# Recurrent stage in two halves: two branch products, a gate chunk, half the recurrent gates, then the other half; second root behind two silus

## The chip, the core and the metric

The kernel runs on one core of a Trainium2 chip. The metric is the device time of one execution in microseconds; less is better. The core has five engines that run side by side, each working through its own list of instructions in order: TensorE (PE in the profile, matmuls; PEld is its weight load), ScalarE (ACT), VectorE (DVE), GpSimd (POOL) and SyncE (SP, which here only issues transfers). They meet at semaphores: an instruction can wait until a semaphore has reached a value, and everything behind it on its engine waits too. Weights come from HBM into SBUF by DMA, matmuls write into eight PSUM banks of 128x512 floats.

## The reference, cut to what matters

The program computes two transformer-like blocks over 256 tokens of width 1024. The change touches only the last mixer, a gated linear recurrence, and what surrounds it:

```python
mod = c_act @ ada_w[layer] + ada_b[layer]                  # shift, scale, gate
h = rmsnorm(x, norm_g[layer]) * (1.0 + scale) + shift
proj = h @ w_in                                            # 1024 -> 2048
xr, gate = proj[..., :1024], proj[..., 1024:]
xc = conv_b + sum(xp[:, j:j + S] * conv_w[j] for j in range(4))      # causal, 4 taps
r = sigmoid(xblk @ w_a + b_a)                              # 8 blocks of 128x128
i = sigmoid(xblk @ w_x + b_x)
log_a = -8.0 * r * softplus(-lam)
a = exp(log_a)
u = sqrt(-expm1(2.0 * log_a)) * (i * xc)
hs[t] = a[t] * hs[t - 1] + u[t]                            # the recurrence over tokens
y = (hs * silu(gate)) @ w_out
x = x + gate_of_the_layer * y                              # then the last rmsnorm
```

## The kernel before, in words

Activations lie with the 1024 features on partitions, as eight tiles of 128 features x 256 tokens; a "half" of the recurrent stage is four such tiles. Every float32 product is made of three matmuls on a high and a low part (`feature_product`, L516; `token_product`, L522).

**Weights.** `weight_stream` (L115) lists chunks in the order of use. A chunk is two units of 128x1024 floats (128x512 for `wax`, which holds the block weights of the recurrent gates). SyncE loads chunk n into one of three raw slots once VectorE has made both low parts of chunk n-3 (L425). ScalarE copies each unit to its high part (`ahead`, L938, instruction L945), VectorE subtracts to get the low part (`ahead`, L1387, instruction L1392). Six units fit in the rings, so unit v waits until TensorE has used unit v-6. `product(key)` on either engine first makes five units more than that chunk and then waits until TensorE has used the chunk. So where a call of `ahead` or `product` stands in an engine's list says when the weights of later chunks are made.

**The stage in question** begins at L903 for TensorE. Numbered by chunks, TensorE does: four branch products `xr` 0 to 3 (48 matmuls each, `columns_chunk`), the recurrent gates of the first half (`gates(0)`, 24 matmuls over four banks), gate chunk `l_gate` 0, `gates(1)`, `l_gate` 1, 2 and 3, and then the output projection `lru_o` (L652): five feature tiles of 12 matmuls of 512 columns, a `fold` (four matmuls, L562) in banks 0 and 1, and the last three tiles. The projection asks for `o_ready` before tiles 0, 2, 4 and 6.

ScalarE (L1312 to L1371): for each branch product two scalings from PSUM (L1316) and, when VectorE has done the convolution, the high part (L1324); then for each half eight sigmoids (L1340), tanh and two exps (`decay`, L1326); both square roots (L1348); four silus of the gate chunks (L1354) with the high parts of the gated result between and behind them (L1359). It loads an activation table when the function needs another one: sigmoid and tanh share one, exp, sqrt and silu have their own.

VectorE (L1948 to L2002): for each branch product six convolution steps (L1957), the low part of the branch (`xc_low`, L1942), and a `modulate` (L1422, work for the layer's gate); then for each half four scalings of the rates (L1976) and the ratio (L1980); then by quarters the input product (L1989, once per half), two scans (L1991), the product with the silu (L1997) and its low part (`o_low`, L1911), which raises `o_ready`. GpSimd multiplies the input gate with the branch (L504), once per half.

## Time and profile before

| | |
|---|---|
| median of three runs | 982.44 us (979.80 to 984.41) |
| profiled execution | 984.87 us, of which the span of the trace is 983.1 us |
| TensorE matmul busy | 840.7 us, 86% of the span |
| VectorE / ScalarE / GpSimd busy | 743.7 / 519.3 / 74.6 us |
| mean granted TensorE clock | 0.954 of full speed |

The page gives for each engine its busy time, for groups of instructions their mean duration and the idle time just before them with what ended it, and a chain of work that is followed back from the last instruction. Times within the span are counted from its start. PEclk is the granted TensorE clock: 1.00 is 2.4 GHz, 0.50 is 1.2 GHz. The recurrent stage lies between 877 and 975 us of the span.

### The profile page before, as it was taken

Reading aid. Unit: us, or ns where it says so; the run is one execution under the profiler, and the core shown is the slowest. Engines: PE = TensorE matmul, PEld = TensorE weight load, DVE = VectorE, ACT = ScalarE, POOL = GpSimd, SP = SyncE. Lnnn points to the kernel's source line nnn. Section 1 sums busy time; section 2 is a strip of 40 time slices with the busy share of each in tenths; the row PEclk is TensorE's granted clock in tenths of the full one; section 3 lists DMA queues with packets and bytes.
Section 4 is the critical chain, followed back from the end, with each engine's and each line's share of the span. In section 5 each row is a group of like instructions: output and inputs, shape, how many; then the busy total and the mean of one; then the engine's idle time right before and its main releaser. Section 6 shows DMA issues by size and latency. Waiting matters only on the chain.

```text
span 983.1 us, 14674 instructions
## 1 busy us (share of the span) xinstructions
PE 840.7 (86%) x5608; PEld 765.5 (78%) x5608; DVE 743.7 (76%) x1153; ACT 519.3 (53%) x892; POOL 74.6 (8%) x118
## 2 busy tenths in 40 slices
PE   0378797999999989996989999999499789889846
PEld 0377676999999969994788998999399668879835
DVE  3889777787878867897578876867778755779675
ACT  0345656544545475447483525544455676464962
POOL 1000010010000000004000040000100000000100
PEclk9798999999999989998999999999699899999978
DMA  8877644778788649986447899875288411556411
GB/s 330 279 241 267 227 161 153 239 239 309 266 316 303 239 146 316 378 320 208 172 150 255 301 177 323 276 254 174 87 273 304 172 43 64 176 169 220 156 75 43
DMA packets 122677, 216.29 MB, mean 220 GB/s; under 512 B 12235, under 2 KB 97975, under 8 KB 115440
## 3 DMA queue, kind: packets, MB, share of 16 engines
q1 hardware_dynamic: 106828, 134.79, 40.5%
q0 software_dynamic: 12960, 72.46, 21.7%
q10 hardware_dynamic: 2820, 8.11, 2.5%
q8 instruction: 45, 0.74, 0.3%
q14 instruction: 24, 0.20, 0.1%
HBM read 214.18 MB, written 1.15 MB: 219 GB/s over the span
## 4 chain that ended last, share of the span: by engine, by line
PE 55%; DVE 23%; ACT 11%; issue 5%; DMA 5%; SPq 0%; DVEq 0%; ACTq 0%
PE bank L518 10%; PE bank L519 10%; PE bank L520 10%; PE bank L524 6%; DVE w_lo L1392 6%; PE bank L525 6%; PE bank L526 6%; DVE modsum L1422 3%; ACT w_hi L945 2%; DMA raw<-in_mod_w 2%; DMA raw<-in_ffn_w_in 2%; PE bank L573 1%; DVE of L1422 1%; DVE kk L1957 1%; PE bank L619 1%
## 5 line engine op out<-in xcount | busy, mean ns | idle before, releaser
L1392 DVE TENSOR_TENSOR w_lo<-raw,w_hi 128x1024 fp32r<-128x1024 f32 (+2 forms) x250 | 292.6, 1207 | 105.7 <-ACT w_hi L945 105.3
L518 PE MATMUL bank<-h_hi,w_hi 128*128 128x256 f32 (+2 forms) x1184 | 340.5, 288 | 13.9 <-DVE h_lo L1545 4.9
L519 PE MATMUL bank<-h_lo,w_hi 128*128 128x256 f32 (+2 forms) x1184 | 337.8, 285 | 0.0
L520 PE MATMUL bank<-h_hi,w_lo 128*128 128x256 f32 (+2 forms) x1184 | 337.5, 285 | 0.0
L945 ACT ACTIVATE w_hi<-raw 128x1024 fp32r<-128x1024 f32 (+2 forms) x250 | 249.6, 1031 | 124.4 <-PE bank L526 48.7
L518 PEld LDWEIGHTS bank<-h_hi,w_hi 128*128 128x128 f32 (+2 forms) x1184 | 228.8, 193 | 18.8 <-issue 15.2
L519 PEld LDWEIGHTS bank<-h_lo,w_hi 128*128 128x128 f32 (+2 forms) x1184 | 228.9, 193 | 1.4 <-issue 0.5
L520 PEld LDWEIGHTS bank<-h_hi,w_lo 128*128 128x128 f32 (+2 forms) x1184 | 228.9, 193 | 0.2
L524 PE MATMUL bank<-w_hi,o_hi 128*128 128x512 f32 x312 | 125.2, 401 | 15.1 <-DVE o_lo L1911 14.0
L525 PE MATMUL bank<-w_lo,o_hi 128*128 128x512 f32 x312 | 122.6, 393 | 0.0
L526 PE MATMUL bank<-w_hi,o_lo 128*128 128x512 f32 x312 | 122.3, 392 | 0.0
L1422 DVE SCALAR_TENSOR_TENSOR modsum<-modraw,small,modsum 128x2048 f32<-128x2048 f32 (+1 forms) x38 | 81.7, 2151 | 5.1 <-DMA modraw<-in_mod_w 2.5
L524 PEld LDWEIGHTS bank<-w_hi,o_hi 128*128 128x128 f32 x312 | 59.5, 191 | 28.2 <-ACT kk L1354 14.2
L526 PEld LDWEIGHTS bank<-w_hi,o_lo 128*128 128x128 f32 x312 | 59.1, 190 | 12.8
L525 PEld LDWEIGHTS bank<-w_lo,o_hi 128*128 128x128 f32 x312 | 59.3, 190 | 11.9 <-issue 0.7
L459 POOL DMA_DIRECT2D modraw<-in_mod_w x52 | 27.9, 538 | 388.7 <-DVE modsum L1422 136.2
L1130 ACT ACTIVATE kk<-kk 128x512 f32<-128x512 f32 x22 | 13.9, 633 | 76.2 <-DVE kk L1693 76.2
L459 POOL DMA_DIRECT2D modraw<-in_ada_w x32 | 17.1, 535 | 395.9 <-DVE modsum L1422 190.5
L1422 DVE SCALAR_TENSOR_TENSOR of<-modraw,small,of 128x2048 f32<-128x2048 f32 (+1 forms) x21 | 41.9, 1995 | 3.4 <-PE bank L520 2.2
L1136 ACT ACTIVATE o_hi<-kk 128x512 fp32r<-128x512 f32 x22 | 13.9, 632 | 45.3 <-DVE kk L1697 45.3
L619 PE MATMUL bank<-cst,prob 128*128 128x128 f32 x96 | 19.6, 321 | 18.4 <-ACT prob L1094 18.4
L1125 ACT ACTIVATE kk<-bank,cols 128x256 f32<-128x256 f32 x44 | 22.4, 559 | 24.3 <-PE bank L520 24.0
(268 smaller groups left out, 1122.8 us busy)
## 6 DMA issues: line engine op xcount, KB each, us to landing
raw<-in_ffn_w_in SPq DMA_DIRECT2D x88, 512.0 KB, 6.1
modraw<-in_mod_w POOLq DMA_DIRECT2D x36, 1024.0 KB, 6.7
raw<-in_ffn_w_out SPq DMA_DIRECT2D x44, 512.0 KB, 7.3
modraw<-in_ada_w POOLq DMA_DIRECT2D x16, 1024.0 KB, 5.4
raw<-in_attn_w_in SPq DMA_DIRECT2D x26, 512.0 KB, 5.8
raw<-in_moba_w_in SPq DMA_DIRECT2D x24, 512.0 KB, 9.4
modraw<-in_mod_w POOLq DMA_DIRECT2D x16, 512.0 KB, 4.3
modraw<-in_ada_w POOLq DMA_DIRECT2D x16, 512.0 KB, 5.3
```

What stands on the lines that cost most here:

```text
L459: pool.dma_start(modraw[:, slot, at:at + src.shape[1]], src).then_inc(sem(f"mod_in{slot}"), 16)
L518: pe.matmul(dst, cut(hi(u)), a_hi, start=first, stop=False, skip_group_check=True)
L519: pe.matmul(dst, cut(hi(u)), a_lo, start=False, stop=False, skip_group_check=True)
L520: return pe.matmul(dst, cut(lo(u)), a_hi, start=False, stop=last, skip_group_check=True)
L524: pe.matmul(dst, a_hi, cut(hi(u)), start=first, stop=False, skip_group_check=True)
L525: pe.matmul(dst, a_hi, cut(lo(u)), start=False, stop=False, skip_group_check=True)
L526: return pe.matmul(dst, a_lo, cut(hi(u)), start=False, stop=last, skip_group_check=True)
L619: ins = pe.transpose(b[:, i * P:(i + 1) * P], prob[:, (g % SD) * CAUSAL + i * P:(g % SD) * CAUSAL + (i + 1) * P], ident)
L945: act.activation(hi(v), raw_unit(v), ACT.Copy).then_inc(sem("w_hi_ready"), 1)
L1125: act.activation(tiles(conv, s, s + 1), bank[0][:, t * S:(t + 1) * S], ACT.Identity, bias=cb[:, f:f + 1], scale=w2[:, 2 * FT + f:2 * FT + ...
L1392: dve.tensor_tensor(lo(v), raw_unit(v), hi(v).bitcast(F32), ALU.subtract).then_inc(sem("w_lo_ready"), 1)
L1422: ins = dve.scalar_tensor_tensor(acc, src, ck, acc, ALU.mult, ALU.add)
```

## The change

In `weight_stream` the order of the chunks becomes xr 0, xr 1, l_gate 0, wax 0, xr 2, xr 3, l_gate 1, wax 1, l_gate 2, l_gate 3. TensorE follows that order, with other banks for the gates and other waits. ScalarE and VectorE take the first half (branches 0 and 1, gates, decay, root, scans) before or between the parts of the second. On ScalarE the root of the first half now stands between branches 2 and 3, and the root of the second half behind silus 0 and 1 and two high parts, ahead of silus 2 and 3: nine table loads in the stage where there were seven. The calls of `ahead` move with it. On VectorE the scans of a half come in one go. The `fold` of the projection now also needs silu 3, since its banks are those of gate chunks 2 and 3. No instruction that computes is added or removed.

```diff
--- before.py
+++ after.py
@@ -168,13 +168,14 @@
         cols(("a_gate", m), ain, 2312 + m * 256)
     rows2("attn_o", w["attn_w_out_2"][0])
     lin = w["lru_w_in_2"][0]
-    for m in range(4):
-        cols(("xr", m), lin, m * 256)
     a_and_x = [w[f"lru_w_{name}_2"][0].rearrange("n w v -> w n v") for name in ("a", "x")]
     for i in range(2):
+        for m in (2 * i, 2 * i + 1):
+            cols(("xr", m), lin, m * 256)
+        cols(("l_gate", i), lin, 1024 + i * 256)
         out.append((("wax", i), [(src[:, 4 * i:4 * i + 4], 0) for src in a_and_x], 128))
-        for m in ((0,), (1, 2, 3))[i]:
-            cols(("l_gate", m), lin, 1024 + m * 256)
+    for m in (2, 3):
+        cols(("l_gate", m), lin, 1024 + m * 256)
     rows2("lru_o", w["lru_w_out_2"][0])
     return out
 
@@ -390,8 +391,8 @@
         turn_keys += [("l_gate", m) for m in range(4)]
         turn_of = {key: n for n, key in enumerate(turn_keys)}
 
-        gate_banks = [[(4, 5), (6, 7)], [(1, 2), (3, 4)]]
-        l_gate_banks = [0, 5, 6, 2]
+        gate_banks = [[(5, 6), (7, 1)], [(3, 5), (6, 7)]]
+        l_gate_banks = [4, 2, 0, 1]
 
         def early_slot(n):
             return raw[:, n - MODRAW, :] if n < MODRAW + RAW else vv[:, 0:2048]
@@ -660,6 +661,8 @@
                             pe.wait_ge(sem("o_ready"), ready[6 + t])
                         ins = row_block(u0 + kt, (o_hi, o_lo), kt, t, h, kt == 0, False)
                     ins.then_inc(sem("w_used"), 1)
+                if name == "lru_o":
+                    pe.wait_ge(sem("turn_read"), turn_of[("l_gate", 3)] + 1)
                 if g is not None:
                     fold(g, (0, 1), parts)
                 for kt in range(KT - TAIL, KT):
@@ -900,9 +903,6 @@
             norm_turns(5)
 
 
-            for m in range(4):
-                key = ("xr", m)
-                end_chunk(columns_chunk(key, turn(key), (h_hi, h_lo), e=None if m else 5))
             def gates(i):
                 for j in range(2):
                     u = unit0("wax", i) + j
@@ -916,18 +916,25 @@
                                               tiles(o_lo, n, n + 1), True, True)
                     ins.then_inc(sem("w_used"), 1)
 
+            for m in (0, 1):
+                key = ("xr", m)
+                end_chunk(columns_chunk(key, turn(key), (h_hi, h_lo), e=None if m else 5))
+            end_chunk(columns_chunk(("l_gate", 0), bank[l_gate_banks[0]], (h_hi, h_lo)))
             gates(0)
+            for m in (2, 3):
+                if m == 3:
+                    pe.wait_ge(sem("rg_read"), 8)
+                key = ("xr", m)
+                end_chunk(columns_chunk(key, turn(key), (h_hi, h_lo), e=None))
             pe.wait_ge(sem("turn_read"), turn_of[("xr", 0)] + 1)
-            end_chunk(columns_chunk(("l_gate", 0), bank[l_gate_banks[0]], (h_hi, h_lo)))
+            end_chunk(columns_chunk(("l_gate", 1), bank[l_gate_banks[1]], (h_hi, h_lo)))
+            pe.wait_ge(sem("turn_read"), turn_of[("xr", 1)] + 1)
+            gates(1)
             pe.wait_ge(sem("turn_read"), turn_of[("xr", 3)] + 1)
-            pe.wait_ge(sem("rg_read"), 2)
-            gates(1)
-            pe.wait_ge(sem("rg_read"), 8)
-            end_chunk(columns_chunk(("l_gate", 1), bank[l_gate_banks[1]], (h_hi, h_lo)))
             end_chunk(columns_chunk(("l_gate", 2), bank[l_gate_banks[2]], (h_hi, h_lo)))
+            end_chunk(columns_chunk(("l_gate", 3), bank[l_gate_banks[3]], (h_hi, h_lo)))
             pe.wait_ge(sem("rg_read"), 16)
-            end_chunk(columns_chunk(("l_gate", 3), bank[l_gate_banks[3]], (h_hi, h_lo)))
-            pe.wait_ge(sem("turn_read"), turn_of[("l_gate", 2)] + 1)
+            pe.wait_ge(sem("turn_read"), turn_of[("l_gate", 1)] + 1)
             out_projection("lru_o", 10)
 
 
@@ -1309,7 +1316,7 @@
             gate_bias(5)
 
 
-            for m in range(4):
+            def branch(m):
                 b = turned(("xr", m))
                 for t in range(2):
                     f = 2 * m + t
@@ -1332,7 +1339,7 @@
                 act.wait_ge(sem("decay_exp"), 2 * i + 1)
                 act.activation(tiles(qz, a, b), tiles(qz, a, b), ACT.Exp).then_inc(sem("decay_exp"), 1)
 
-            for i in range(2):
+            def gates_out(i):
                 product("wax", i)
                 for j, (dst, pb) in enumerate(((qz, "b_a"), (vv, "b_x"))):
                     for k in range(4):
@@ -1340,10 +1347,8 @@
                         act.activation(tiles(dst, n, n + 1),
                                        bank[gate_banks[i][j][k // 2]][:, (k % 2) * S:(k % 2 + 1) * S], ACT.Sigmoid,
                                        bias=pcol[pb][:, n:n + 1]).then_inc(sem("rg_read"), 1)
-                ahead(unit0("l_gate", i) + AHEAD)
-                decay(i)
-                ahead(unit0("l_gate", i) + 1 + AHEAD)
-            for i in range(2):
+
+            def input_root(i):
                 act.wait_ge(sem("ratio_ready"), i + 1)
                 act.activation(tiles(of, 4 * i, 4 * i + 4), tiles(of, 4 * i, 4 * i + 4), ACT.Sqrt,
                                scale=-1.0).then_inc(sem("input_root"), 1)
@@ -1359,13 +1364,29 @@
                 act.activation(tiles(o_hi, 2 * m, 2 * m + 2), tiles(kk, 2 * m, 2 * m + 2), ACT.Copy).then_inc(
                     sem("o_hi_ready"), 1)
 
+            branch(0)
+            branch(1)
+            ahead(unit0("l_gate", 0) + AHEAD)
+            gates_out(0)
+            decay(0)
+            branch(2)
+            input_root(0)
+            branch(3)
+            ahead(unit0("l_gate", 1) + AHEAD)
+            gates_out(1)
+            ahead(unit0("l_gate", 2) + AHEAD)
+            decay(1)
+            ahead(unit0("l_gate", 2) + 1 + AHEAD)
             gate_out(0)
             gate_out(1)
+            gated_high(0)
+            gated_high(1)
+            ahead(unit0("l_gate", 3) + AHEAD)
+            input_root(1)
             gate_out(2)
-            gated_high(0)
             gate_out(3)
-            for m in range(1, 4):
-                gated_high(m)
+            gated_high(2)
+            gated_high(3)
             sqrt_table()
             ahead(last_unit[5] + TAIL)
             rms_norm(6, 5)
@@ -1945,7 +1966,7 @@
                                   tiles(o_hi, 2 * m, 2 * m + 2).bitcast(F32), ALU.subtract).then_inc(
                                       sem("xc_ready"), 1)
 
-            for m in range(4):
+            def branch(m):
                 product("xr", m)
                 b = bank[turn_of[("xr", m)] % 4]
                 for j in (2, 1, 0):
@@ -1963,42 +1984,67 @@
                             ins.then_inc(sem("xc_full"), 1)
 
                 dve.nop().then_inc(sem("turn_read"), 1)
-                if m:
-                    xc_low(m - 1)
-                modulate(1)
-            xc_low(3)
-            for i in range(2):
-                a, b = 4 * i, 4 * i + 4
-                ahead(unit0("wax", i) + 1 + AHEAD)
+
+            def rates(i):
                 for k in range(4):
                     n = 4 * i + k
                     dve.wait_ge(sem("rg_read"), 8 * i + k + 1)
                     dve.tensor_scalar(tiles(qz, n, n + 1), tiles(qz, n, n + 1), lam8[:, n:n + 1], None,
                                       ALU.mult).then_inc(sem("rate_ready"), 1)
-                ahead(unit0("l_gate", i) + AHEAD)
+
+            def ratio(i):
+                a, b = 4 * i, 4 * i + 4
                 dve.wait_ge(sem("decay_exp"), 2 * i + 2)
                 dve.scalar_tensor_tensor(tiles(of, a, b), tiles(of, a, b), 1.0, tiles(bias, a, b), ALU.add,
                                          ALU.mult).then_inc(sem("ratio_ready"), 1)
-                ahead(unit0("l_gate", i) + 1 + AHEAD)
-            ahead(unit0("l_gate", 2) + AHEAD)
-            for m in range(4):
-                if m % 2 == 0:
-                    a, b = 2 * m, 2 * m + 4
-                    dve.wait_ge(sem("input_root"), m // 2 + 1)
-                    dve.wait_ge(sem("ix_ready"), m // 2 + 1)
-                    link(dve.tensor_tensor(tiles(vv, a, b), tiles(vv, a, b), tiles(of, a, b), ALU.mult))
-                for n in (2 * m, 2 * m + 1):
+
+            def scans(i):
+                a, b = 4 * i, 4 * i + 4
+                dve.wait_ge(sem("input_root"), i + 1)
+                dve.wait_ge(sem("ix_ready"), i + 1)
+                link(dve.tensor_tensor(tiles(vv, a, b), tiles(vv, a, b), tiles(of, a, b), ALU.mult))
+                for n in range(a, b):
                     dve.tensor_tensor_scan(tiles(bias, n, n + 1), tiles(qz, n, n + 1), tiles(vv, n, n + 1), 0.0,
                                            ALU.mult, ALU.add).then_inc(sem("scanned"), 1)
-                if m in (1, 2):
-                    ahead(unit0("l_gate", 2) + m + AHEAD)
+
+            def gated_rows(m):
                 dve.wait_ge(sem("turn_read"), turn_of[("l_gate", m)] + 1)
                 dve.wait_ge(sem("scanned"), 2 * m + 2)
                 dve.tensor_tensor(tiles(kk, 2 * m, 2 * m + 2), tiles(kk, 2 * m, 2 * m + 2),
                                   tiles(bias, 2 * m, 2 * m + 2), ALU.mult).then_inc(sem("l_gated"), 1)
-                if m:
-                    o_low(kk, m - 1, 20)
-            o_low(kk, 3, 20)
+
+            branch(0)
+            modulate(1)
+            branch(1)
+            xc_low(0)
+            modulate(1)
+            xc_low(1)
+            rates(0)
+            ahead(unit0("l_gate", 0) + 1 + AHEAD)
+            branch(2)
+            ratio(0)
+            xc_low(2)
+            modulate(1)
+            branch(3)
+            xc_low(3)
+            modulate(1)
+            scans(0)
+            ahead(unit0("l_gate", 1) + AHEAD)
+            rates(1)
+            ahead(unit0("wax", 1) + 1 + AHEAD)
+            ratio(1)
+            ahead(unit0("l_gate", 2) + AHEAD)
+            gated_rows(0)
+            gated_rows(1)
+            o_low(kk, 0, 20)
+            o_low(kk, 1, 20)
+            ahead(unit0("l_gate", 2) + 1 + AHEAD)
+            scans(1)
+            ahead(unit0("l_gate", 3) + AHEAD)
+            for m in (2, 3):
+                gated_rows(m)
+            for m in (2, 3):
+                o_low(kk, m, 20)
             out_projection("lru_o", lambda i: fold(10, (0, 1)) if i == 2 else None)
             rms_norm(6, 5)
             dve.wait_ge(sem("final_in"), 16)
```

## Rows read from the trace of the kernel before

**Rows 1.** The page: the chain that ended last, by engine.

```profile
PE 55%; DVE 23%; ACT 11%; issue 5%; DMA 5%; SPq 0%; DVEq 0%; ACTq 0%
```

**Rows 2.** Busy time by stretch; behind POOL: PEclk, DMA share, GB/s.

```profile
877.00:903.00 26.00, 25.43 (x198) 25.33 (x198) 24.35 (x42) 15.23 (x28) 1.06 (x2) 0.93 0.55 172
...
912.00:936.00 24.00, 20.67 (x168) 20.30 (x168) 16.21 (x18) 23.81 (x34) 4.83 (x2) 1.00 0.49 175
936.00:949.30 13.30, 0.00 (x0) 0.00 (x0) 7.92 (x12) 10.15 (x13) 0.00 (x0) 0.63 0.22 81
949.30:975.00 25.70, 25.59 (x100) 20.04 (x100) 18.12 (x25) 7.94 (x14) 0.00 (x0) 0.92 0.00 1
975.00:983.10 8.10, 0.00 (x0) 0.00 (x0) 4.35 (x8) 1.15 (x5) 0.00 (x0) 0.63 0.35 129
```

**Rows 3.** Waits from 877 to 950: total us, times, longest.

```profile
ACT o_hi L1324 <- DVE kk L1957: 14.1, 4, 4.0
...
DVE w_lo L1392 <- ACT w_hi L945: 9.8, 4, 5.2
```

**Rows 4.** Timeline of ScalarE: start, duration (all of them together), what, count.

```profile
911.38 1.28 ACT L1340 ACT_TABLE_LOAD   x1
912.68 1.57 ACT L1340 ACTIVATE qz<-bank,cols 128x256 f32<-128x256 f32 x4
...
915.55 1.11 ACT L945 ACTIVATE w_hi<-raw 128x1024 fp32r<-128x1024 f32 x1
916.50 1.11 ACT L1329 ACTIVATE bias<-qz 128x1024 f32<-128x1024 f32 x1
917.62 1.28 ACT L1331 ACT_TABLE_LOAD   x1
...
920.01 1.06 ACT L1333 ACTIVATE qz<-qz 128x1024 f32<-128x1024 f32 x1
920.97 2.94 ACT L945 ACTIVATE w_hi<-raw 128x1024 fp32r<-128x1024 f32 x3
...
939.18 1.09 ACT L1354 ACTIVATE kk<-bank 128x512 f32<-128x512 f32 x2
940.15 2.00 ACT L945 ACTIVATE w_hi<-raw 128x1024 fp32r<-128x1024 f32 x2
```

**Rows 5.** Timeline of VectorE, same columns.

```profile
893.52 2.94 DVE L1957 SCALAR_TENSOR_TENSOR kk<-bank,cols,kk 128x255 f32<-128x255 f32 x6
896.37 0.68 DVE L1944 TENSOR_TENSOR o_lo<-kk,o_hi 128x512 fp32r<-128x512 f32 x1
896.97 1.28 DVE L1422 SCALAR_TENSOR_TENSOR vv<-modraw,small,vv 128x1024 f32<-128x1024 f32 x1
...
916.69 2.60 DVE L1392 TENSOR_TENSOR w_lo<-raw,w_hi 128x1024 fp32r<-128x1024 f32 x1 [2.05 <-ACT w_hi L945]
...
922.24 3.49 DVE L1392 TENSOR_TENSOR w_lo<-raw,w_hi 128x1024 fp32r<-128x1024 f32 x3
...
942.39 1.22 DVE L1989 TENSOR_TENSOR vv<-vv,of 128x1024 f32<-128x1024 f32 x1
943.64 1.27 DVE L1991 TENSOR_TENSOR_SCAN bias<-qz,vv 128x256 f32<-128x256 f32 x2
945.01 0.69 DVE L1997 TENSOR_TENSOR kk<-kk,bias 128x512 f32<-128x512 f32 x1
```

**Rows 6.** TensorE at the projection's start, from the timeline.

```profile
949.36 0.77 PE L524 MATMUL bank<-w_hi,o_hi 128*128 128x512 f32 x1 [14.01 <-DVE o_lo L1911]
```

**Rows 7.** The granted clock in windows of 2 us, columns as in Rows 2.

```profile
939.00:941.00 2.00, 0.00 (x0) 0.00 (x0) 0.00 (x0) 1.99 (x4) 0.00 (x0) 0.64 0.00 0
...
951.00:953.00 2.00, 2.00 (x6) 1.52 (x6) 2.00 (x4) 0.00 (x0) 0.00 (x0) 0.50 0.00 0
953.00:955.00 2.00, 2.00 (x10) 1.66 (x9) 2.00 (x4) 0.63 (x1) 0.00 (x0) 0.95 0.00 0
```

**Rows 8.** Raw weight transfers between 845 and 983, issue to landing.

```profile
DMA to landing us min/median/max: 2.9/4.7/7.2
```

## Prediction

> **What bounds the kernel now.** I read the page's chain first, then busy time by stretch, then waits and timelines of the last 110 us. Over the whole span the chain is mostly TensorE [rows 1], but that average doesn't hold where the change is made. Four stretches are to be told apart [rows 2]. From 877 to 903 TensorE and VectorE are both full, with the branch products and convolutions. From 912 to 936 ScalarE is full (23.81 of 24.00 us). From 936.0 to 949.3 TensorE does nothing, while ScalarE is busy for 10.15 us and VectorE for 7.92. From 949.3 to 975 the projection keeps TensorE full, and 8.1 us of norm and store follow, which the change doesn't touch. The first matmul of the projection had stood idle for 14.01 us, waiting for a low part of the gated result [rows 6]. What made that late is ScalarE's list: both halves of gates, decays and roots, and only then the silus at 939.18 [rows 4]; VectorE waits for it too (9.8 us in four waits for high parts of weights [rows 3]) and makes input product, scans and gated product from 942.39 on [rows 5]. ScalarE in turn loses 14.1 us earlier, in four waits for convolutions [rows 3]. So the price of the stage is the way through ScalarE and VectorE, not TensorE's work.
>
> **What the change does with that.** No computing instruction goes or comes. The first half's gates come before branches 2 and 3, so part of ScalarE's work moves into its early waits. I lay the new lists end to end, each instruction starting when the one before it on its engine and what it waits for are done. Steps from start to start, out of the rows: ScalarE 0.95 us for a high part, 0.53 taken for a 512-wide one (an estimate, half the columns and some overhead), eight sigmoids 2.87, tanh 0.96, second exp 0.96, silu 0.49; a table load costs 1.41, that is 1.28 to 1.30 for itself and 0.1 by which the instruction ahead of it drains longer (tanh takes 1.12 to the load, where others of its size take 0.95); load and first exp take 2.39, with the drain 2.5 [rows 4]. VectorE: six convolution steps 2.87, branch low part 0.60, modulate 1.2, low part of a weight unit 1.14 (3.49 for three), input product 1.25, scan 0.60, gated product 0.60 [rows 5]. TensorE: 0.12 us for a 256-wide matmul at full clock (25.43 us x 0.93 / 198 [rows 2]), 0.23 for a 512-wide one, and twice that at half [rows 7].
>
> First half. Unit 6 is now a 512-wide one, so the second convolution ends at 895.8 instead of 896.4. VectorE then does a low part, a modulate and a low part: 898.2. The remaining 18 gate matmuls end at 900.6. ScalarE: table and sigmoids 4.3, tanh 0.96, table and exps 3.5, to 909.4; high parts 13 and 14 to 910.9. VectorE: low part 14 to 912.2, convolution to 915.1, ratio to 916.2. ScalarE: root table and root 2.4, high parts 15 and 16 to 920.2. VectorE: low part 16 and the last convolution to 924.4. ScalarE: branch high part to 925.0, four high parts (17 to 20) to 928.8.
>
> What is hidden there. VectorE now waits for the first sigmoids (902.5) before it makes low part 9, and 9 to 12 are queued behind that: TensorE stands 1.9 us in branch product 2, but that product is ready at 908 and VectorE comes to it at 912, so nothing is lost. The wait for all eight sigmoids before branch 3 is over at 904.9, three us early. GpSimd's product (L504) now overlaps low part 10, where the one beside it before took 2.60 us instead of 1.2 [rows 5]; VectorE later waits 1.9 us for high part 13, which covers the 1.4. In the second half it overlaps parts 19 and 20, ahead of a wait of 3 us for the exps. GpSimd's last two modulation transfers go out when modulates 1 and 2 are done, ahead of its products, as before. Transfers: the wax 1 chunk is sent when low part 9 is made, at 905.0; it is needed at 910.3 by high part 14. With the median landing of 4.7 us, and 0.45 to issue, that just fits; at the longest, 7.2, it costs 2.5, at the shortest nothing [rows 8]. The other transfers have over 3 us to spare.
>
> Second half. The last branch low part is there at 925.8. TensorE has stood since 920.4, for 5.4 us, in the middle of `gates(1)`. This is the first cost that before doesn't show: its long idle was 14.01 us, in which the clock fell to half some 4.3 us in (939 to 941 has 0.64), and it came back 3.9 us after the restart, in the window from 953 [rows 6, 7]. At full clock the 18 matmuls end at 928.1 and hide behind the high parts; at half they take 4.3 and end at 930.0, which costs ScalarE 1.3. The idles between 912 and 936, 3.3 us in all, brought no fall (20.67 us busy of 24.00, clock 1.00 [rows 2]). 5.4 is nearer to the 4.3 at which it fell than to that, so I take the fall: both ends, 0 and 1.3, stay in the range. From 930.0 ScalarE: table and sigmoids 4.3, high part 0.95, tanh 0.96, table and exps 3.5, high part 0.95, silu table and two silus 2.4: 943.1. Gated products and high parts of quarters 0 and 1 alternate with VectorE to 944.6, then high part 23, root table, root: 947.9. VectorE: input product 1.25, four scans 2.4, low part 23, two gated products 1.2, two low parts behind their high parts 1.4, low part 24 with its end 1.23: 956.6. TensorE begins the projection at 944.9, does tiles 0 to 3 in 10.9 and stands 0.9 for low part 24. From 956.6: tile 4 2.7, fold 1.9, last three tiles 36 x 0.2265 + 0.2 = 8.3: 969.6. Before that end was at 975.0 [rows 2]. **The sum is -5.3 us.** The same laying out, done with before's lists, ends at 974.9, so the durations carry.
>
> The two added table loads are on this way: one root load ahead of branch 3, one second silu load in place of a shared one. They are in the sum at 1.41 each. The Trainium skill, ScalarE: Activation LUTs, What ACT_TABLE_LOAD costs, has 1.28 us for the load plus 1.38 of drain, 2.66 for each switch. The trace agrees with the first and not with the second: the load at 917.62 follows a tanh that began 1.12 before [rows 4].
>
> The profiled execution took 984.87 us for a span of 983.1; less 5.3 that is 979.6. It lies 2.4 above the median of the runs, so against 982.44 the change gives **977.1 us**.
>
> **Rivals.**
> No fall of the clock before the second half of the gates: -6.6, 975.8. For it: the idle is barely over what it took to fall. Chance 0.20.
> A second fall, at the projection: TensorE stands 3.4 us ahead of it. At half for 4 us it loses 2.0, for 7 us 3.3, of which 0.9 is hidden: -4.2 to -2.9, near 978.9. For it: the earlier stall falls in the same stretch. Against: 3.4 is under 4.3. Chance 0.18.
> The wax 1 transfer lands late: up to 2.5 more, -2.8, 979.6. VectorE's waits for the first sigmoids set its start. Chance 0.08.
> A table switch costs more here than in its rows: if ScalarE ran empty for as long as the load takes (1.28 us in place of 0.1 [rows 4]), the two added ones bring 2.4 more, -2.9, 979.5. No row shows it. Chance 0.04. By the drain that the Trainium skill, ScalarE: Activation LUTs, gives, it would be this case.
> Slower: the clock stays at half through the projection. TensorE then pays 0.20 more for each of 96 matmuls of 512 columns [rows 7]; with 0.9 of slack, 31 of them eat the 5.3 and 55 make it slower by over 0.5%; all of them give +12.8, 990. Against: before, full clock was back nine matmuls after 14 us of idle. Chance 0.04.
> The hand-offs between ScalarE and VectorE cost more than before's rows (ten in the way, each some tenths), -3 to 0: near 980.5. Chance 0.10.
>
> **How the numbers follow.** The forecast, 977.1, has 0.36. A measurement of this kernel tells about 0.5% (4.9 us) from no change; the forecast is barely over that and the runs of before spread by 4.6, so it counts 0.55 to 0.45. Faster: 0.20 from the forecast, 0.17 of the first rival, 0.08 of the second and third together: 0.45. Slower: the clock rival's 0.03 and 0.02 of the hand-offs. The rest, 0.50, is no change. Range: down to the first rival with 2 us of spread between medians (973.8), up to the late ones with the same (982.0).
>
> **What would show it.** Right: the wait for `o_ready` ahead of the projection falls from 14 us to under 5; TensorE's first 512-wide matmul is near 945 and its last near 970; an idle of about 5 us inside the second gates; ScalarE with nine loads from 900 to 955; low part 24, not a low part of the result, released the fifth tile. Wrong: ScalarE idle for long ahead of `hi` of wax 1; the first matmul of the projection after 947; half clock beyond 935; a branch 3 that is done after 926.

## The result, and the profile after

| | before | changed |
|---|---|---|
| median of 8 runs each | 984.38 us (979.80 to 986.29) | 976.22 us (973.32 to 980.15) |
| ratio of the changed kernel to before | | 0.9924 (95% interval 0.9901 to 0.9948) |
| profiled execution, its span | 984.87, 983.1 us | 980.15, 978.3 us |
| stage: first branch matmul to last matmul of the projection | 877.57 to 974.96: 97.39 us | 879.49 to 970.24: 90.75 us |

The change makes the kernel faster by 7.5 us (5.1 to 9.7 by the interval), 0.8%. The forecast was 5.3 us, 977.1. Between the two profiled executions the span fell by 4.8 us, and the stage by 6.64: the changed kernel's execution came to the stage 1.92 us later, though the code ahead of it is the same. The start of the stage lies between 872.88 and 879.49 in the twelve traces of this study, so the stage's own length is the measure for small effects, and it is used in all that follows. No kernel was traced twice, so how far this length varies by itself isn't measured; differences of 0.1 or 0.2 us are not read as effects. The first rows bound that stage in the changed kernel; they are TensorE's timeline (start, duration, what, and in brackets the idle before it and what ended it):

```profile
879.49 0.36 PE L519 MATMUL bank<-h_hi,w_hi 128*128 128x256 f32 x1 [0.94 <-DVE h_lo L1566]
...
927.02 0.58 PE L519 MATMUL bank<-o_hi,w_hi 128*128 128x256 f32 x1 [4.79 <-DVE o_lo L1965]
...
944.85 0.72 PE L525 MATMUL bank<-w_hi,o_hi 128*128 128x512 f32 x1 [2.05 <-DVE o_lo L1932]
...
969.85 0.39 PE L527 MATMUL bank<-w_hi,o_lo 128*128 128x512 f32 x1
```

The 14.01 us ahead of the projection [rows 6] have become 2.05, and 4.79 stand inside the second gates, where the low part of branch 3 is waited for. Busy time by stretch, for [rows 2]:

```profile
877.00:903.00 26.00, 23.84 (x181) 23.28 (x182) 20.60 (x36) 18.39 (x30) 1.05 (x2) 0.93 0.65 202
...
912.00:936.00 24.00, 19.21 (x145) 19.01 (x144) 22.07 (x34) 17.18 (x27) 1.55 (x1) 0.86 0.48 159
...
943.00:949.00 6.00, 4.15 (x11) 3.33 (x12) 4.42 (x6) 5.68 (x7) 0.00 (x0) 0.72 0.51 175
949.00:969.50 20.50, 20.50 (x88) 16.25 (x88) 16.29 (x23) 9.53 (x16) 0.00 (x0) 1.00 0.00 1
```

The stretch without any matmul is gone. ScalarE, which was full from 912 to 936, now has slack there too (17.18 of 24.00), and VectorE carries more (22.07 us, before 16.21). The clock column has 0.93 at the start of the stage, as before, and two new falls: one in the second gates and one at the start of the projection. In windows of 2 us the first of them, which ends after 930:

```profile
924.00:926.00 2.00, 0.00 (x0) 0.00 (x0) 1.51 (x4) 0.39 (x1) 0.00 (x0) 0.61 0.63 258
926.00:928.00 2.00, 0.98 (x4) 0.98 (x5) 1.72 (x2) 2.00 (x3) 0.00 (x0) 0.50 0.00 0
928.00:930.00 2.00, 2.00 (x12) 2.00 (x11) 1.97 (x4) 2.00 (x3) 0.00 (x0) 0.50 0.00 0
930.00:932.00 2.00, 2.00 (x14) 2.00 (x14) 2.00 (x5) 1.97 (x4) 0.00 (x0) 0.69 0.00 0
```

ScalarE over the second gates and the silus, for [rows 4], with its waits for the convolutions first, for [rows 3]:

```profile
ACT o_hi L1331 <- DVE kk L1978: 13.5, 4, 3.5
...
925.61 0.63 ACT L1331 ACTIVATE o_hi<-kk 128x512 fp32r<-128x512 f32 x1 [3.24 <-DVE kk L1978]
926.15 3.88 ACT L952 ACTIVATE w_hi<-raw 128x1024 fp32r<-128x1024 f32 x4
930.05 1.28 ACT L1347 ACT_TABLE_LOAD   x1
931.35 1.57 ACT L1347 ACTIVATE qz<-bank,cols 128x256 f32<-128x256 f32 x4
...
940.70 1.28 ACT L1359 ACT_TABLE_LOAD   x1
941.99 1.09 ACT L1359 ACTIVATE kk<-bank 128x512 f32<-128x512 f32 x2
943.35 1.23 ACT L1364 ACTIVATE o_hi<-kk 128x512 fp32r<-128x512 f32 x2 [0.27 <-DVE kk L2013]
...
945.54 1.28 ACT L1353 ACT_TABLE_LOAD   x1
946.84 1.06 ACT L1353 ACTIVATE of<-of 128x1024 f32<-128x1024 f32 x1
947.91 1.28 ACT L1359 ACT_TABLE_LOAD   x1
```

To compare with the laying out of the prediction, which began at before's 877.57, take 1.92 from these times. Three things are to be seen. The four waits for convolutions are nearly as long as before (13.5 us, before 14.1). The table load at 930.05 did not wait: the last of the second gates' matmuls ended at 931.23, the load had begun ahead of the wait, and the sigmoid followed at 931.35. And the silus begin at 940.1 (941.99 - 1.92), where the prediction's list has its second silu end at 943.1 and so its first begin at 942.1. VectorE's part, for [rows 5]:

```profile
914.04 2.93 DVE L1978 SCALAR_TENSOR_TENSOR kk<-bank,cols,kk 128x255 f32<-128x255 f32 x6
...
922.65 2.94 DVE L1978 SCALAR_TENSOR_TENSOR kk<-bank,cols,kk 128x255 f32<-128x255 f32 x6
926.28 0.69 DVE L1965 TENSOR_TENSOR o_lo<-kk,o_hi 128x512 fp32r<-128x512 f32 x1 [0.69 <-ACT o_hi L1331]
...
947.92 1.23 DVE L2005 TENSOR_TENSOR vv<-vv,of 128x1024 f32<-128x1024 f32 x1 [1.49 <-ACT of L1353]
949.19 2.44 DVE L2007 TENSOR_TENSOR_SCAN bias<-qz,vv 128x256 f32<-128x256 f32 x4
...
955.26 1.22 DVE L1413 TENSOR_TENSOR w_lo<-raw,w_hi 128x1024 fp32r<-128x1024 f32 x1
```

### The profile page after: what moved, and what is told of

Read it like the earlier page. It is cut to its first block, busy times and chain, and to the rows that moved or that the text cites. A ratio compares the mean times of both kernels' runs of the same rounds, so it can differ in the third digit from the quotient of the medians.

```text
span 978.3 us, 14677 instructions
## 1 busy us (share of the span) xinstructions
PE 847.5 (87%) x5608; PEld 771.3 (79%) x5608; DVE 742.8 (76%) x1153; ACT 521.7 (53%) x894; POOL 78.0 (8%) x118
## 3 DMA queue, kind: packets, MB, share of 16 engines
q0 software_dynamic: 12960, 72.46, 21.8%
HBM read 214.18 MB, written 1.15 MB: 220 GB/s over the span
## 4 chain that ended last, share of the span: by engine, by line
PE 56%; DVE 23%; ACT 10%; issue 5%; DMA 5%; POOLq 1%; SPq 0%; ACTq 0%; DVEq 0%
PE bank L519 10%; PE bank L521 10%; PE bank L520 10%; DVE w_lo L1413 7%; PE bank L525 6%; PE bank L526 6%; PE bank L527 6%; DVE modsum L1443 3%; ACT w_hi L952 2%; DMA raw<-in_mod_w 2%; DMA raw<-in_ffn_w_in 2%; PE bank L574 1%; PE bank L620 1%; DVE of L1443 1%; PE bank L634 1%
## 5 line engine op out<-in xcount | busy, mean ns | idle before, releaser
L1413 DVE TENSOR_TENSOR w_lo<-raw,w_hi 128x1024 fp32r<-128x1024 f32 (+3 forms) x250 | 292.0, 1205 | 96.6 <-ACT w_hi L952 96.1
L952 ACT ACTIVATE w_hi<-raw 128x1024 fp32r<-128x1024 f32 (+3 forms) x250 | 249.5, 1030 | 126.7 <-PE bank L527 49.1
L527 PEld LDWEIGHTS bank<-w_hi,o_lo 128*128 128x128 f32 x312 | 59.1, 190 | 12.8
```

The lines of the kernel that those rows point to most:

```text
L527: return pe.matmul(dst, a_lo, cut(hi(u)), start=False, stop=last, skip_group_check=True)
L952: act.activation(hi(v), raw_unit(v), ACT.Copy).then_inc(sem("w_hi_ready"), 1)
L1413: dve.tensor_tensor(lo(v), raw_unit(v), hi(v).bitcast(F32), ALU.subtract).then_inc(sem("w_lo_ready"), 1)
```

## The experiments

All lengths are of the stage as defined above, each from one profiled execution; where a kernel was also timed, its ratio to before stands beside it. The counts of matmuls in the edits are written out here; in the kernels they are constants.

| kernel | stage, us | against 90.75 | projection begins after |
|---|---|---|---|
| before | 97.39 | +6.64 | 71.79 |
| changed | 90.75 | | 65.36 |
| matmuls inside the second gates (warm_gates) | 90.77 | +0.02 | 65.35 |
| these and some ahead of the projection (warm_both) | 89.99 | -0.76 | 65.37 |
| changed, second root ahead of the silus (root_first) | 93.68 | +2.93 | 67.73 |
| before, second root behind two silus (before_root_late) | 99.75 | +9.00 (+2.36 against before) | 73.18 |
| changed, gate chunk 0 behind the first gates (gate_chunk_behind) | 94.13 | +3.38 | 68.72 |
| changed, low parts 9 and 10 earlier (low_parts_first) | 90.58 | -0.17 | 65.20 |
| changed, two more table loads (extra_tables) | 93.62 | +2.87 | 68.22 |
| changed, ScalarE's waits filled (fill_act) | 88.84 | -1.91 | 64.21 |
| the same with the matmuls (fill_warm) | 87.98 | -2.77 | 63.38 |
| the same with low part 24 earlier (fill_warm_low24) | 87.83 | -2.92 | 63.40 |

### Was the half clock in the second gates on the way?

```diff
                         if j == 0 and k % 2 == 0:
+                            if n == 6:
+                                for _ in range(32):
+                                    pe.matmul(bank[6][:, 0:S], h_hi[:, 0:P], tiles(h_hi, 0, 1), start=True, stop=True)
                             pe.wait_ge(sem("xc_ready"), n // 2 + 1)
```

> The changed kernel with 32 matmuls of 256 columns on unused data put where TensorE stood idle for 4.8 us inside the second gates; their result is overwritten. They take 3.8 us at full clock and end before the low part that the gates wait for. Measure: the length of the stage, from the first branch matmul to the last one of the projection, 90.75 us in the changed kernel. Theory A (the prediction's term): the half clock there costs ScalarE 1.3 us on the way, so the stage is 1.3 shorter, 89.4. Theory B (from the trace of after: the sigmoids' table load at 930.05 ran while ScalarE was waiting for the gates, which ended at 931.23, and the first sigmoid came at 931.35): the load hides the half clock but for 0.1 us, so 90.4 to 90.9. Both expect full clock from 920 to 940.

Measured: 90.77 us. TensorE's idle there was 0.94 us and the clock stayed at full; the busy time from 916 to 936.9, and then ScalarE around the gates:

```profile
916.00:936.90 20.90, 19.25 (x159) 18.87 (x158) 16.69 (x25) 17.57 (x25) 5.16 (x1) 1.00 0.42 147
```

```profile
922.97 3.88 ACT L956 ACTIVATE w_hi<-raw 128x1024 fp32r<-128x1024 f32 x4
926.88 1.28 ACT L1351 ACT_TABLE_LOAD   x1
928.17 1.57 ACT L1351 ACTIVATE qz<-bank,cols 128x256 f32<-128x256 f32 x4
```

The fall is taken away and the stage keeps its length to 0.02 us. From the first of the four high parts to the first sigmoid it is 5.20 us with matmuls at full clock and 5.20 (926.15 to 931.35) with matmuls at half. So theory B holds, and the 1.3 us that the prediction charged for this fall was no cost in this kernel.

### And the one at the projection?

```diff
             pe.wait_ge(sem("rg_read"), 16)
+            for _ in range(14):
+                pe.matmul(bank[7][:, 0:S], h_hi[:, 0:P], tiles(h_hi, 0, 1), start=True, stop=True)
             pe.wait_ge(sem("turn_read"), turn_of[("l_gate", 1)] + 1)
```

> The same, and 14 more such matmuls ahead of the projection, where TensorE stood idle for 2.06 us and then ran its first eight matmuls at half clock. Their price by the rows of after: about 1.7 us of TensorE, of which the fifth tile's wait for the low part of unit 24 (ready at 956.5, wanted at 957.4 at half clock and at 955.7 at full) leaves 0.9. Expected stage: 0.7 to 1.1 shorter than with the gates' matmuls alone, 89.4 to 90.0, and the fifth tile then waits for a low part of a weight. Rival: the second fall is not on the way either, 90.4 to 90.9.

Measured: 89.99 us, 0.78 shorter than with the gates' matmuls alone. The projection begins at the same place, 65.37 into the stage, so all of it lies behind: the first matmuls are no longer at half. In the fifth tile TensorE waited:

```profile
951.33 0.47 PE L527 MATMUL bank<-w_hi,o_hi 128*128 128x512 f32 x1 [0.60 <-issue]
```

That 0.60 is slack that had hidden part of the fall. The size is that of the theory. What released the tile the trace doesn't name, but the low part of unit 24 ended on VectorE at 951.23, 0.1 us before the tile began (950.01 + 1.22), which fits the expectation. This run has both groups of matmuls; since the fall at the projection came with the gates' matmuls alone too (the projection took 25.42 us there, 24.62 here), it doesn't hang on the earlier fall.

### The second root back ahead of the silus

```diff
             ahead(unit0("l_gate", 2) + 1 + AHEAD)
+            input_root(1)
             gate_out(0)
             gate_out(1)
             gated_high(0)
             gated_high(1)
             ahead(unit0("l_gate", 3) + AHEAD)
-            input_root(1)
```

> One part of the change undone: the second half's root ahead of the four silus instead of behind two, one table load fewer in the stage. Theory: the projection starts 2.3 us later (root table 1.3 and root 1.0 now stand ahead of silu 0), but the second quarters come earlier by the 1.4 of the silu load, so the stage is 0.4 to 1.4 longer, 91.2 to 92.2. Rival (tables bound the stage): one load fewer makes it 1.3 shorter, 89.4.

Measured: 93.68 us, ratio to before 0.9966 (0.9945 to 0.9987). The projection:

```profile
945.02 0.77 PE L525 MATMUL bank<-w_hi,o_hi 128*128 128x512 f32 x1 [4.40 <-DVE o_lo L1932]
```

It begins 2.37 us later, as expected. But the stage is 2.93 longer, more than the 0.4 to 1.4: the expectation let the second quarters decide the end, and they don't here. The idle of 4.40 us left the clock at half for the first ten matmuls and part of an eleventh (until 949.7), and four tiles from a start 2.37 us later come to the fifth tile at 80.8 us (67.73, 10.9 for four tiles, 2.2 for the half clock), when its weight's low part had been ready since 77.8 (953.85 + 1.22 - 877.29). So the projection's start decided, and all of the delay counts, with 0.56 more for the longer half clock (the projection took 25.95 us, before this edit 25.39). The rival, that one load fewer pays, is out. This kernel is also the halves without the late root: with 93.68 it is 3.71 us under before, so the halves pay by themselves.

### The same edit alone, on the kernel before

```diff
-            for i in range(2):
+            def input_root(i):
                 act.wait_ge(sem("ratio_ready"), i + 1)
...
+            input_root(0)
...
             gate_out(1)
+            input_root(1)
             gate_out(2)
```

> One part of the change alone: the kernel before with only the second root moved behind silus 0 and 1. Theory: in before the projection waits for quarter 0, whose low part stands on VectorE behind the scans of both quarters and two weight units that ScalarE makes after the silus; the second silu load is added in front of these (1.4) and the root leaves (1.0) and comes back in front of them: 0.5 to 1.5 us longer than before's stage of 97.39. So this part earns nothing without the halves. Rival: it brings the first quarter forward as in the changed kernel, 1 to 2 us shorter.

Measured: 99.75 us, 2.36 longer than before; ratio 1.0026 (1.0006 to 1.0046). ScalarE:

```profile
938.21 1.28 ACT L1356 ACT_TABLE_LOAD   x1
939.51 1.09 ACT L1356 ACTIVATE kk<-bank 128x512 f32<-128x512 f32 x2
940.61 1.28 ACT L1348 ACT_TABLE_LOAD   x1
941.91 1.06 ACT L1348 ACTIVATE of<-of 128x1024 f32<-128x1024 f32 x1
942.87 1.99 ACT L945 ACTIVATE w_hi<-raw 128x1024 fp32r<-128x1024 f32 x2
944.87 1.28 ACT L1356 ACT_TABLE_LOAD   x1
```

```profile
952.05 0.76 PE L524 MATMUL bank<-w_hi,o_hi 128*128 128x512 f32 x1 [15.43 <-DVE o_lo L1914]
```

The root comes out from ahead of the silus, but the two weight units that the projection's first tile waits for stand behind both. The wait grows from 14.01 to 15.43, and the projection itself takes 26.57 us instead of 25.60. The direction is that of the theory, the size is 0.9 over its range; the longer projection accounts for it. Its first 13 matmuls ran at half clock, where before it was eight, and start to start these take 0.43 us instead of 0.23: that is the 0.97. The late root is worth -2.93 us in the halves and +2.36 without them, so it pays only with them; the halves pay 3.71 us without it.

### The gate chunk behind the first gates

```diff
-        cols(("l_gate", i), lin, 1024 + i * 256)
+        if i:
+            cols(("l_gate", i), lin, 1024 + i * 256)
         out.append((("wax", i), [(src[:, 4 * i:4 * i + 4], 0) for src in a_and_x], 128))
+        if not i:
+            cols(("l_gate", i), lin, 1024 + i * 256)
...
-            end_chunk(columns_chunk(("l_gate", 0), bank[l_gate_banks[0]], (h_hi, h_lo)))
             gates(0)
+            end_chunk(columns_chunk(("l_gate", 0), bank[l_gate_banks[0]], (h_hi, h_lo)))
...
             branch(1)
-            ahead(unit0("l_gate", 0) + AHEAD)
             gates_out(0)
```

> One part of the change undone: gate chunk 0 (48 matmuls) behind the first gates instead of ahead of them, in TensorE's order and in the weight stream, with ScalarE's weight unit ahead of the first sigmoids left to a later call. Theory: the first gates wait for VectorE's low parts anyway (until 898.2 in the laying out), so the chunk filled TensorE's time for nothing where it was; behind the gates it pushes branch 2 from 902.5 to 908.3 and its end past the time at which VectorE comes to it: the stage is 1.5 to 3.5 us longer than 90.75 (92.0 with a clock at full, up to 93.6 with a fall in the idle of about 6 us ahead of the first gates). Rival: VectorE comes later still and nothing is lost, 90.7.

Measured: 94.13 us, 3.38 longer. TensorE stands ahead of the first gates, and they run at half clock (895.25 and 895.47 for the second and third, 0.21 to 0.22 us apart instead of 0.12):

```profile
894.90 0.55 PE L522 MATMUL bank<-o_hi,w_hi 128*128 128x256 f32 x1 [5.95 <-DVE o_lo L1967]
...
895.47 0.41 PE L524 MATMUL bank<-o_hi,w_lo 128*128 128x256 f32 x1
```

A high part on ScalarE then waits 2.58 us for them (at 898.35). At the upper end of what was expected. So the gate chunk's place, with that of the weight unit that moved along, is worth 3.4 us: it takes TensorE's time where that is free, and with it there the clock stayed up. How much of the 3.4 is the clock's was not tried apart.

### The low parts ahead of the first sigmoids

```diff
             xc_low(1)
+            ahead(unit0("xr", 2) + 2)
             rates(0)
```

> The changed kernel with the low parts of units 9 and 10 on VectorE ahead of its wait for the first sigmoids instead of behind it. It takes away TensorE's idle of 1.39 us in branch product 2 and sends the wax 1 transfer some 2 us earlier. Theory: both are off the way, the stage stays at 90.5 to 90.9. Rival (the prediction's third one, a transfer that lands late): ScalarE's high part 14 waited for it, and the stage is 0.5 to 1.5 shorter.

Measured: 90.58 us. TensorE's idle of 1.39 us in branch 2 is gone and 1.42 us more are at the second gates, 6.21 instead of 4.79: it was hidden, and so was the transfer. The wax 1 transfer was issued 21.8 us into the stage instead of 27.3, so 5.5 us earlier and not 2, and still the stage changed by 0.17 only, far from the rival's 0.5 to 1.5. In the changed kernel itself ScalarE went from high part 13 to 14, which reads that transfer, without a gap (at 911.01).

### What a table load costs on the way

```diff
                 act.activation(tiles(bias, a, b), tiles(qz, a, b), ACT.Tanh).then_inc(sem("rate_tanh"), 1)
+                sqrt_table()
                 act.wait_ge(sem("rate_tanh"), i + 1)
```

> The disputed cost by itself: in each of the two decays a root of one column between tanh and the exps, so ScalarE loads the root table and then the exp table: one load and one activation of 0.2 us more in each half, both on the way. Theory from the rows (a load is 1.28 us and its drain 0.1): about 1.6 each, the stage 3.0 to 3.6 longer, 93.7 to 94.4; up to 1.4 more if the clock falls for longer. Rival (a switch costs 2.66 us with its drain, as the Trainium skill, ScalarE: Activation LUTs, has it): 2.9 each, 5.7 longer, 96.4.

Measured: 93.62 us, 2.87 longer, 1.44 for each load with its activation, just under the 3.0 to 3.6 of the theory and far from the rival's 5.7. ScalarE in the first half:

```profile
904.92 1.28 ACT L976 ACT_TABLE_LOAD   x1
906.22 0.20 ACT L976 ACTIVATE nstat<-ones 128x1 f32<-128x1 f32 x1
906.42 1.28 ACT L1339 ACT_TABLE_LOAD   x1
907.72 1.06 ACT L1339 ACTIVATE of<-qz 128x1024 f32<-128x1024 f32 x1
```

From one load to the next it is 1.50 us. The drain of 1.38 us that the Trainium skill, ScalarE: Activation LUTs, What ACT_TABLE_LOAD costs, adds to each switch isn't there; the load's 1.28 is. The measurement decides: the prediction's fourth rival is out.

### ScalarE's waits filled

```diff
+                if m:
+                    ahead((unit0("xr", 2) + 2, unit0("l_gate", 2), unit0("l_gate", 3) + 1)[m - 1])
                 act.wait_ge(sem("xc_full"), 2 * m + 2)
```

> Not a part of the change, but a test of what bounds it: ScalarE makes the high parts of later weight units (9 and 10, 15 and 16, 17 to 19) while it waits for the convolutions of branches 1, 2 and 3, where it stands idle 3.2 to 3.5 us each, instead of behind them. Same instructions, other places. Theory (the way runs through ScalarE's list): the stage is 1.1 to 3.1 us shorter, 87.7 if the clock stays at full in the second gates, up to 89.6 with two falls, since the second gates then wait for TensorE and no table load hides the half clock. Rival (VectorE's list bounds the stage): 90.5 to 90.9.

Measured: 88.84 us, 1.91 shorter, inside the theory's range. Around the second gates ScalarE now waits:

```profile
916.58 2.95 ACT L952 ACTIVATE w_hi<-raw 128x1024 fp32r<-128x1024 f32 x3
920.29 0.63 ACT L1333 ACTIVATE o_hi<-kk 128x512 fp32r<-128x512 f32 x1 [0.76 <-DVE kk L1980]
923.45 1.06 ACT L952 ACTIVATE w_hi<-raw 128x1024 fp32r<-128x1024 f32 x1 [2.53 <-PE bank L521]
924.52 1.28 ACT L1349 ACT_TABLE_LOAD   x1
925.95 1.57 ACT L1349 ACTIVATE qz<-bank,cols 128x256 f32<-128x256 f32 x4
```

The wait for the last convolution has shrunk from 3.24 us to 0.76 (all four from 13.5 to 7.3), and the way now goes through TensorE's gates, which ran at half clock. Of the 1.91 us, 1.15 are an earlier start of the projection. The other 0.76 are the projection itself, 24.63 us instead of 25.39: TensorE stood 1.41 us ahead of it and its clock stayed at full, so the fall that cost 0.78 above went away by itself. So with this edit the clock in the second gates should come onto the way. Both groups of matmuls go in again, 14 ahead of the projection, and in the second gates fewer than in the first experiment:

```diff
-                                for _ in range(32):
+                                for _ in range(22):
```

> The kernel with ScalarE's weight units in its waits for the convolutions, and with the matmuls on unused data (22 inside the second gates, 14 ahead of the projection). In fill_act the second gates followed a TensorE idle of 3.69 us at half clock, high part 20 waited 2.53 us for them, and the first sigmoid came 1.4 us after the table load had begun. Theory: here, other than in the changed kernel, TensorE's clock is on the way: the stage is 87.5 to 88.1, against 88.84 without these matmuls. Rival: another wait takes the place and it stays at 88.6 to 89.

Measured: 87.98 us, 0.86 shorter; median 972.24 us, ratio to before 0.9875 (0.9857 to 0.9894). Nearly all of it is an earlier start of the projection (64.21 to 63.38, 0.83 us), which the matmuls inside the gates had moved by 0.01 in the changed kernel. The last edit:

```diff
             for m in (2, 3):
                 gated_rows(m)
+            ahead(unit0("lru_o", 2))
             for m in (2, 3):
```

> The same, and the low part of unit 24 on VectorE ahead of the last two low parts of the result, since the fifth tile of the projection waited for it (0.6 us in warm_both). The fifth tile then waits for the low part of quarter 2 instead, 0.6 us earlier. Expected stage: 0.3 to 0.6 shorter than the kernel without this edit, 87.0 to 87.7; against before a ratio of 0.988 to 0.991. Rival: TensorE is itself the bound by then and it changes nothing.

Measured: 87.83 us, 0.15 shorter; median 973.51 us, ratio 0.9884 (0.9867 to 0.9901). That is less than the 0.3 to 0.6 expected, and the intervals of the two lie over each other: no gain to be told. The wait of 0.60 us at the fifth tile is gone, but the last three tiles now stand for the low parts of their weights:

```profile
955.19 0.47 PE L527 MATMUL bank<-w_hi,o_hi 128*128 128x512 f32 x1 [0.30 <-DVE w_lo L1422]
```

Both kernels beat before. Against the changed one (0.9924, 0.9901 to 0.9948), the one without the last edit has a ratio whose interval lies wholly under; the interval of the one with it just meets that of the changed kernel.

## Why the prediction was right, step by step

**Direction and range.** Faster was forecast, with 977.1 us in a range of 973.8 to 982.0; 976.22 was measured. The outcome, faster by over 0.5%, had 0.45, and no change had 0.50. That 977.1 lies within 1 us of the measured median is partly luck. The forecast started from 982.44 for before, the median of three runs, and eight runs gave 984.38; it took off 5.3, and the ratio puts the gain at 7.5 us. A base that was 1.9 too low and a gain that was 2.2 too small nearly made up for each other. The gain itself was forecast at 70% of its size.

**Where the time went.** The prediction has part of ScalarE's work move into its early waits. These waits hardly shrank, from 14.1 us [rows 3] to 13.5. From the start of the stage to the first matmul of the projection ScalarE was busy for 54.23 us and idle for 17.56 before, and busy for 50.86 and idle for 14.50 in the changed kernel. So of the 6.43 us by which the projection starts earlier in the stage, 3.4 are work that now stands behind its start (mostly the second half's root and silus 2 and 3), and 3.1 are idle time, about as much as before's wait of 3.10 for the first gated product. VectorE's idle time in the same stretch fell from 14.82 to 10.17 us. The laying out end to end had this right; the sentence about the waits had not.

**The first half** held to a few tenths. With 1.92 taken off, the convolution of branch 1 ended at 895.8 (predicted 895.8), that of branch 2 began at 914.04 - 1.92 = 912.1 (912.2), and the idle of branch 2 was 1.39 us (1.9) and off the way, as low_parts_first shows. Inside it one price was off without effect: low part 11 on VectorE took 3.43 us beside GpSimd's product, 2.2 more than usual where 1.4 had been charged, and that used up the 1.9 us of waiting that was to hide it.

**The term that was wrong: table loads behind a wait.** The prediction put the root's and the sigmoids' load behind the wait for their operand. In the trace both run ahead of it: the root's at once behind the high part of branch 2 (0.6 us gained), the sigmoids' while the gates still ran (1.4 us gained). Together they are 2.0 us: the first sigmoid came at 931.35 - 1.92 = 929.4, where 930.0 + 1.4 was predicted, and the silus are early by as much. The same made the fall of the clock in the second gates free: it came as predicted, in an idle of 4.79 us (5.4 predicted), but cost nothing (warm_gates), where 1.3 had been charged.

**A second fall** came too, which the forecast had as a rival with 0.18. Its reason for it, the earlier stall, is not the cause: with that fall taken away (warm_gates) the second one stayed. Its reason against it, that 3.4 us is under 4.3, failed: the fall came behind an idle of 2.05. Taking it away gave 0.78 us (warm_both), where the rival had 1.1 to 2.4 net. So the sum of the parts: 5.3 forecast, 2.0 more for the loads, 0.8 less for the second fall comes to 6.5, against 6.64 measured.

**What bounds the changed kernel** ahead of the projection is still ScalarE's list. Filling its waits brings the projection forward by 1.15 us, and 0.76 more come from a clock that then stayed up (fill_act); after that TensorE's clock in the second gates counts as well.

**The other rivals.** No fall of the clock: refuted by the trace. A late transfer: no wait for it in the trace, and the stage changed by 0.17 us when it was sent 5.5 us earlier. A dearer table switch: refuted by extra_tables. Clock at half through the projection: it was back after eight matmuls. The 990 that the prediction gives for this rival is a slip: +12.8 against before's 982.44 is 995. Dearer hand-offs: with the loads put right, the laying out leaves 0.1 us for all of them.

**The signs.** Met: the wait ahead of the projection under 5 us (2.05), the first matmul of the projection near 945 (944.85) and the last near 970 (969.85), an idle of about 5 us in the second gates, nine loads between 900 and 955. Not met: low part 24 released nothing in the changed kernel, since it was ready at 956.48 and the fifth tile, late by the second fall, began at 957.43. And one sign of being wrong came: half clock beyond 935, that same fall. The two times near 945 and 970 hold in the trace as it is; counted from before's start of the stage they are 942.9 and 968.3, early by what the loads gave.

**Open.** The stage's 6.64 us lie inside the interval of the ratio (5.1 to 9.7), so nothing beyond them has to be explained. Whether the code ahead of the stage, which is the same, runs a little sooner because one of the stage's first four chunks, which are loaded there, is now a small one, isn't settled: the stage begins at 877.57 and 878.87 in the two kernels with the old order, and between 872.88 and 879.49 in the ten with the new one.

## What to carry to other kernels

Where one engine has its waits early and its work late, moving half of the dependent work up between the waits can pay, here 6.64 us of a wait of 14.01. It pays by what no longer stands ahead of the next engine's start, and the waits themselves may stay. Laying the lists out end to end, in each engine's own order, gave the size here to within a microsecond and a half. The worth of a part depends on the others: the late root gave 2.9 us with the halves and cost 2.4 without, while the halves gave 3.7 without it. Before charging a slower clock, look at what the next engine does meanwhile; here a table load hid all of one fall, and a wait in the projection's fifth tile hid about half of the other.

## What the runs showed of the hardware

A table load on ScalarE started as soon as the engine was free, although the activation behind it had to wait (930.05 against gates that ended at 931.23; again at 924.52, with the sigmoid at 925.95). It cost 1.28 us and about 0.1 of drain. With an activation of one column it was 1.50 us on the engine and 1.44 in the length of the stage (extra_tables).

The granted clock fell within idles of 4.79, 5.95, 4.40 and 3.69 us that followed a full TensorE, and just behind one of 2.05 us ahead of the projection of the changed kernel. With 1.28 us in its place (warm_both) it stayed at full, and with 1.41 (fill_act) too. In between, the length of the idle doesn't tell. The clock stayed at full around idles of 1.95 us in before (at 911.66) and 1.94 in before_root_late, and it fell just behind 1.90 us in low_parts_first and 1.1 us behind one of 1.93 in gate_chunk_behind:

```profile
938.08 0.47 PE L525 MATMUL bank<-w_hi,o_hi 128*128 128x512 f32 x1 [1.90 <-DVE o_lo L1932]
```

Two small groups of matmuls whose results are thrown away were enough to keep it at full in warm_both.

GpSimd's product of 1024 columns took 3.38 and 5.17 us in the changed kernel, where it took 2.42 and 2.41 before. Beside the first one, six low parts on VectorE took 8.58 us together and one of them 3.43 where it usually takes 1.2:

```profile
905.54 8.58 DVE L1413 TENSOR_TENSOR w_lo<-raw,w_hi 128x1024 fp32r<-128x1024 f32 x6
907.81 3.43 DVE L1413 TENSOR_TENSOR w_lo<-raw,w_hi 128x1024 fp32r<-128x1024 f32 x1
...
933.86 3.50 DVE L1413 TENSOR_TENSOR w_lo<-raw,w_hi 128x1024 fp32r<-128x1024 f32 x3
```

```profile
906.77 3.38 POOL L505 TENSOR_TENSOR vv<-vv,kk 128x1024 f32<-128x1024 f32 x1 [6.39 <-ACT vv L1347]
934.45 5.17 POOL L505 TENSOR_TENSOR vv<-vv,kk 128x1024 f32<-128x1024 f32 x1 [24.30 <-ACT vv L1347]
```

The times add up as if one of the two stood while the other ran. In the first half the product, started at 906.77, got under way when the low part before it ended at 907.8 and was done at 910.15, and the long low part ended 1.1 us later, at 911.24. In the second half GpSimd gave way: three low parts took their usual 3.50 us, to 937.4, and the product was done 2.3 us after them. In before a low part of 2.60 us ended 1.1 us behind the product beside it. The prediction had VectorE pay in both halves; what decides which of the two pays no run here tried.
